# A depthwise convolution's taps, moved between two ways of feeding the matrix engine

## The reference

```
h = x + 0.5 * swiglu(rms(x), ffn1)
u = rms(h) @ w_in  ->  q, k, v, c, g
y_attn = window_attention(norm(q), norm(k), v, sink, rel_bias) @ w_attn_out
c = c_val * sigmoid(c_gate)                       # 512 channels
c = depthwise_conv(c, conv_w, conv_b)             # 31 taps along the tokens
c = silu(layer_norm(c));  y_conv = c @ w_conv_out
h = h + (sigmoid(g_a) * y_attn + sigmoid(g_c) * y_conv) @ w_o
h = h + 0.5 * swiglu(rms(h), ffn2);  x = h + (p @ w_pe_proj) * sigmoid(rms(h) @ w_pe_gate)
```

## Time and profile before

| | |
|---|---|
| three runs | 2152.19, 2153.51, 2154.12 us, median 2153.51 |
| the profiled execution | 2154.34 us, span 2152.5 us |
| TensorE busy | 2126.8 us, 99% of the span |
| VectorE busy | 1679.8 us, 78% |
| ScalarE busy | 1264.2 us, 59% |
| weight blocks | 664 of 512 KB |
| granted TensorE clock | 1.000 |

### The profile page before, as it was taken

One profiled execution on the slowest core, in us unless ns is written; L12 is line 12 of the kernel. 1 busy time (PEld: TensorE's weight loads), 2 busy tenths in 40 slices (PEclk: granted clock), 3 DMA queues, 4 the chain that ended last, 5 costly groups with the idle time before them and its releaser, 6 DMA issues.

```text
span 2152.5 us, 38861 instructions
## 1 busy us (share of the span) xinstructions
PE 2126.8 (99%) x16094; PEld 1940.7 (90%) x16094; DVE 1679.8 (78%) x2638; ACT 1264.2 (59%) x2114; POOL 13.4 (1%) x20
## 2 busy tenths in 40 slices
PE   8999999999999999999999999999999999999999
PEld 6898989999998899998888999888898889998888
DVE  7888699888877688776886677887688766978875
ACT  4755545555755655555655567666575645766554
POOL 0000000000000000000000000000000000000000
PEclk9999999999999999999999999999999999999999
DMA  9554476767644477555555533555555553345553
GB/s 365 198 194 168 162 252 251 246 233 278 225 155 173 148 245 236 190 183 186 182 190 187 176 118 128 202 190 187 190 180 187 189 190 131 120 166 205 190 191 129
DMA packets 116371, 415.12 MB, mean 193 GB/s; under 512 B 13105, under 2 KB 16561, under 8 KB 115682
## 3 DMA queue, kind: packets, MB, share of 16 engines
q1 hardware_dynamic: 116194, 412.63, 55.7%
HBM read 409.42 MB, written 3.16 MB: 192 GB/s over the span
## 4 chain that ended last, share of the span: by engine, by line
PE 91%; ACT 4%; DVE 3%; DMA 2%; issue 1%; SPq 0%; ACTq 0%; DVEq 0%
PE bank L198 90%; ACT arena L250 2%; DMA raw<-W 1%; DVE arena L205 1%; ACT hi L250 1%; DVE lo L205 1%; PE bank L202 1%; DVE ada L222 0%; ACT L250 0%; ACT L242 0%; DMA xT<-x 0%; DVE arena L213 0%; DVE h L205 0%; SPq L195 0%; DVE ysl L205 0%
## 5 line engine op out<-in xcount | busy, mean ns | idle before, releaser
L198 PE MATMUL bank<-h,hi 128*128 128x256 f32 (+1 forms) x5344 | 1223.1, 314 | 0.0
L250 ACT ACTIVATE hi<-raw 128x1024 fp32r<-128x1024 f32 x656 | 688.9, 1056 | 565.0 <-PE bank L198 501.5
L198 PE MATMUL bank<-h,lo 128*128 128x256 f32 x3440 | 986.1, 287 | 3.8 <-DVE h L205 3.7
L198 PEld LDWEIGHTS bank<-h,hi 128*128 128x128 f32 x5344 | 880.1, 190 | 67.1 <-issue 2.6
L205 DVE TENSOR_TENSOR lo<-raw,hi 128x1024 fp32r<-128x1024 f32 x656 | 793.1, 1221 | 90.4 <-ACT hi L250 89.7
L198 PEld LDWEIGHTS bank<-h,lo 128*128 128x128 f32 x3440 | 654.6, 190 | 15.6 <-issue 7.0
L198 PE MATMUL bank<-act,hi 128*128 128x512 f32 x1056 | 370.0, 393 | 0.0
L198 PE MATMUL bank<-act,lo 128*128 128x256 f32 x1056 | 294.7, 279 | 0.0
L198 PEld LDWEIGHTS bank<-act,hi 128*128 128x128 f32 x1056 | 197.9, 187 | 47.0
L198 PEld LDWEIGHTS bank<-act,lo 128*128 128x128 f32 x1056 | 197.9, 187 | 0.0
L250 ACT ACTIVATE arena<-arena 128x256 f32<-128x256 f32 (+4 forms) x202 | 98.6, 493 | 158.5 <-DVE arena L205 151.0
(11 more groups left out here) (150 smaller groups left out, 1894.0 us busy)
## 6 DMA issues: line engine op xcount, KB each, us to landing
raw<-W SPq DMA_DIRECT2D x664, 512.0 KB, 3.3
ada<-WA SPq DMA_DIRECT2D x80, 512.0 KB, 3.8
arena<-WA SPq DMA_DIRECT2D x16, 512.0 KB, 14.3
p_projected<-arena SPq DMA_DIRECT2D x2, 1024.0 KB, 7.5
arena<-scr SPq DMA_DIRECT2D x16, 128.0 KB, 4.9
arena<-p_projected SPq DMA_DIRECT2D x2, 1024.0 KB, 4.7
xT<-x SPq DMA_DIRECT2D x2, 512.0 KB, 5.2
arena<-lora SPq DMA_DIRECT2D x2, 512.0 KB, 9.6
```

Of the source, the lines that this page charges most:

```text
L198: return self.done(lambda e: e.matmul(out, l, r, start=start, stop=stop, skip_group_check=True))
L250: return self.done(lambda e: e.activation(out, in_, f, scale=scale, **kw))
```

## The change

The 44 float32 tap matmuls of a layer become 44 streamed tiles: each diagonal is laid out beforehand in the weight stream (5.5 more blocks a layer, 11 in all, 675 instead of 664), is split into high and low like any other tile, and makes three matmuls against the high part `Ch` and low part `Cl` of the convolution's input (266 columns, of which each tap reads 256 from its own offset). `tap halves` makes these copies: ScalarE `Ch`, VectorE `Cl`, channel tiles 0 and 1 ahead of c 3, tiles 2 and 3 behind gate2 2. The tiles of the first two channel tiles are a new item on TensorE behind rcol (a tiny item between c 3 and qkv), those of the other two follow gate2 3. ScalarE's building of diagonals goes. VectorE's 80 taps are spread over 24 ticks (4, 3, 3 and again) instead of 20, and one more empty tick stands ahead of the mean. On ScalarE the attention's chain, which ran behind the convolution's in a tick, now runs ahead of it.

```diff
-NT2 = 2 * (44 * 8 + 22 * 8) + 30 * 8 + 32 + 32 + 64 + 64 + 16
+NT2 = 2 * (44 * 8 + 22 * 8) + 30 * 8 + 32 + 32 + 64 + 64 + 16 + 4 * 11
 def conv2_steps(l):
-    s = []
+    s, n = [], 0
     for pair in (0, 2):
-        todo = [(m, j) for m in (pair, pair + 1) for j in range(CV, CW)]
-        built = []
-        for j in range(0, CV, 2):
-            s += [("taps", pair, j)]
-            if j >= 4:
-                s += [("pe tap", pair, *t) for t in built.pop(0)]
-            built.append(todo[:3])
-            del todo[:3]
-            s += [("diag", pair, *t) for t in built[-1]] + ["next"]
+        for size in (4, 3, 3) * 4:
+            s += [("taps", pair, n, n + size), "next"]
+            n += size
+        n = 0
         s += [("conv sum", pair)]
-    return s + ["next", ("mean",), "next", ("square",), "next", ("var",), "next", ("norm",), ("silu",), "next", ("split",)]
+    return s + ["next", "next", ("mean",), "next", ("square",), "next", ("var",), "next", ("norm",), ("silu",), "next", ("split",)]
...
-        s += [("mixer2", l), ("c", l, 0), ("c", l, 1), ("c", l, 2), ("conv2", l), ("c", l, 3), ("c last", l), ("rcol", l)]
+        s += [("mixer2", l), ("c", l, 0), ("c", l, 1), ("c", l, 2), ("conv2", l), ("tap halves", l, (0, 1)), ("c", l, 3),
+              ("c last", l), ("rcol", l), ("taps", l, 0)]
         s += [("qkv", l, p) for p in range(3)] + [("v2", l), ("qk norm", l), ("attention2", l)]
-        s += [("gate2", l, p) for p in range(8)] + [("gate2 last", l), ("finish", ("att2", l))]
+        s += [("gate2", l, p) for p in range(3)] + [("tap halves", l, (2, 3)), ("gate2", l, 3), ("taps", l, 2)]
+        s += [("gate2", l, p) for p in range(4, 8)] + [("gate2 last", l), ("finish", ("att2", l))]
...
+                elif what == "taps":
+                    l, pr = q
+                    o = take(CONV, ("conv", l, pr))
+                    for m in (pr, pr + 1):
+                        pe.wait_ge(v_cv, ("tap halves", l, m))
+                        for j in range(CV, CW):
+                            wh, wl, ends = tile([("conv_w_2", l, j, ("diag", m))])
+                            om = t256(o, m - pr)
+                            ch, cl = (x[m % 3][:, j - CV:j - CV + 256] for x in (Ch, Cl))
+                            pe.mm(om, wl, ch, j == CV, False)
+                            pe.mm(om, wh, ch, False, False)
+                            i = pe.mm(om, wh, cl, False, j == CW - 1)
...
+                        v.tt(Cl[m % 3], Cb[:, m, CV:CV + TW], Ch[m % 3].bitcast(F32), SUB).then_inc(v_cv, ("tap halves", l, m))
...
-                        a.act(diag[n % 8], C("ident"), ACT.Identity, scale=P("conv_w_2", l, j * 4 + m)).then_inc(
-                            a_cv, ("diag", l, m, j))
...
+                        a.act(Ch[m % 3], Cb[:, m, CV:CV + TW], ACT.Copy).then_inc(a_cv, ("tap high", l, m))
...
-                    f.chain(("att2", q[0]), att2_steps(q[0]), attention2(q[0]), True)
+                    f.chain(("att2", q[0]), att2_steps(q[0]), attention2(q[0]))
```

More of the change, by code:

```diff
@@ L1040, in conv2 @@
             def conv2(l):
-                taps = [0]
                 def step(what, *q):
-                    if what == "pe tap":
-                        pr, m, j = q
-                        if (m, j) == (pr, CV):
-                            take(CONV, ("conv", l, pr))
-                        d = diag[taps[0] % 8]
-                        taps[0] += 1
-                        pe.wait_ge(a_cv, ("diag", l, m, j))
-                        pe.wait_ge(v_main, ("c", l, m))
-                        pe.mm(t256(ps(("conv", l, pr)), m - pr), d, Cb[:, m, j:j + 256], j == CV, j == CW - 1).then_inc(
-                            pe_cv, ("tap", l, m, j))
-                    elif what == "mean":
+                    if what == "mean":
                         o = take(CONV, ("cmean", l))
@@ L1240, in tensor_program @@
                     f.chain(item, conv2_steps(q[0]), conv2(q[0]))
+                elif what == "taps":
[10 more added lines that the diff above has]
+                            i = pe.mm(om, wh, cl, False, j == CW - 1)
+                            names = ends + ([("conv", l, pr)] if (m, j) == (pr + 1, CW - 1) else [])
+                            if names:
+                                i.then_inc(pe_main, *names)
+                            if ends:
+                                f.tick()
                 elif what == "c":
@@ L1660, in step @@
                     if what == "taps":
[L1661 to L1671 removed]
+                        pr, first, last = q
+                        for n in range(first, last):
+                            j, m = n // 2, pr + n % 2
+                            o = t256(cacc, m)
+                            if j == 0:
+                                v.wait_ge(v_main, ("c", l, m))
+                                x = v.ts(o, Cb[:, m, 0:256], w(m, 0), P("conv_b_2", l, m), MUL, ADD)
+                            else:
+                                v.wait_ge(v_cv, ("tap", l, m, j - 1))
+                                x = v.stt(o, Cb[:, m, j:j + 256], w(m, j), o, MUL, ADD)
+                            x.then_inc(v_cv, ("tap", l, m, j))
                     elif what == "conv sum":
@@ L1674, in step @@
                         o = cacc[:, pr * 256:(pr + 2) * 256]
-                        v.wait_ge(pe_cv, ("tap", l, pr + 1, CW - 1))
+                        v.wait_ge(pe_main, ("conv", l, pr))
                         v.wait_ge(v_cv, ("tap", l, pr + 1, CV - 1))
@@ L1966, in vector_program @@
                     f.chain(item, conv2_steps(q[0]), conv2(q[0]))
+                elif what == "tap halves":
+                    l = q[0]
+                    for m in q[1]:
+                        v.wait_ge(a_cv, ("tap high", l, m))
+                        v.tt(Cl[m % 3], Cb[:, m, CV:CV + TW], Ch[m % 3].bitcast(F32), SUB).then_inc(v_cv, ("tap halves", l, m))
+                elif what == "taps":
+                    f.tiles(2 * (CW - CV))
                 elif what == "qkv":
@@ L2327, in conv2 @@
                 return step
-            conv_taps = [(m, j) for pr in (0, 2) for m in (pr, pr + 1) for j in range(CV, CW)]
             def merge(name, l, m, h):
@@ L2564, in scalar_program @@
                     f.chain(item, conv2_steps(q[0]), conv2(q[0]))
+                elif what == "tap halves":
+                    l = q[0]
+                    for m in q[1]:
+                        a.wait_ge(v_main, ("c", l, m))
+                        if m == 3:
+                            a.wait_ge(pe_main, ("conv", l, 0))
+                        a.act(Ch[m % 3], Cb[:, m, CV:CV + TW], ACT.Copy).then_inc(a_cv, ("tap high", l, m))
+                elif what == "taps":
+                    f.tiles(2 * (CW - CV))
                 elif what == "rcol":
```

27 lines of the change are left out of this document (5 added, 22 removed).

## The result

| | before | after |
|---|---|---|
| median of five runs each | 2153.62 us | 2162.14 us |
| lowest to highest | 2152.19 to 2154.12 | 2162.07 to 2162.97 |
| ratio, with its 95% interval | | 1.0040 [1.0030, 1.0051] |
| the profiled execution; its span | 2154.34; 2152.5 | 2162.12; 2160.3 |
| granted TensorE clock, mean | 1.000 | 0.998 |

The forecast was 2159.0, slower. The direction and the two large waits came out as laid out; two of the waits were smaller than their terms (2.9 us less together), and two costs for which the forecast had nothing, the clock and a wait at `attn out`, made up for it and more. That the total lies only 3 us off is so in part luck: the errors ran against each other.

What follows compares the result with a forecast made beforehand. TensorE, busy 99%, was taken as the bound: profiled 2154.3 - 5.9 (taps) - 1.0 (variance) + 12.4 (four turn waits) = 2159.8, or 2159.0 against the median. Own range 2156 to 2162; 8 in 10: 2147 to 2163.5.

Steps and rivals of the forecast that it cites:

- The taps: On TensorE, 88 float32 taps (37.6 us) become 88 streamed tiles at 0.36 us each (31.7): 5.9 us less.
- Turn 0: First attention transposes on TensorE would wait for ScalarE's scaling: 4.4 us in the first layer, 3.4 in the second.
- Turn 1: Second pair's attention transposes on TensorE would wait 2.1 us in the first layer, 2.5 in the second.
- Var: TensorE's 0.99 us wait at the convolution's variance would shrink to 0.5 per layer, saving 1.0 us in all.
- The clock: Rival, chance 0.10: TensorE's clock halves behind the two waits at turn 0, each costing 2.88 us more; 2165 us.
- no waits: Rival, chance 0.12: the attention's steps come in time, TensorE stays at 99%, gaining 5.9 plus 1.0; 2146.6 us.
- Half the wait: Rival, chance 0.12: exponentials, not VectorE's queue, decide at both reciprocals, leaving 6 to 7 us of waits; 2153 us.

Runs made afterwards that it cites:

- filler: Kernel after plus ten (first layer) and eight (second) matmuls on constants ahead of the wait at turn 0, result overwritten; 2162.53 us, 1.0036 to before.
- halves_early: Kernel after with the copies for channel tiles 2 and 3 made earlier, behind the second qkv item, turns unmoved; 2162.94 us, 1.0042 to before.
- early_filler: halves_early plus nine (first layer) and seven (second) filling matmuls on constants ahead of the wait at turn 0; 2159.46 us, 1.0028 to before.
- old_end: Kernel after with attention's chain last again on ScalarE and one empty tick, not two, ahead of the mean; 2160.68 us, 1.0032 to before.
- before_turn_earlier: Kernel before with one empty tick less between divide and turn, for both pairs; 2170.99 us, 1.0075 to before.
- no_float_taps: Kernel before without its 88 float32 taps and their diagonals, the sum adding a constant tile instead; 2132.39 us, 0.9898 to before.
- later_and_early: Kernel after with turns one tick later and second-pair copies made behind the second qkv item; 2151.68 us, 0.9990 to before.
- turn_later: Kernel after with one more empty tick between divide and turn, for both pairs; 2160.54 us, 1.0026 to before.
- table_moved: later_and_early with ScalarE's early table load moved from behind the square to right ahead of the variance's logarithm; 2148.93 us, 0.9977 to before.

## Why the forecast held, point by point

**The taps.** 0.36 us a tile, as the distance of high parts in the earlier trace rows had said; TensorE's busy time fell by 2.9 rather than 5.9; the slowed matmuls are counted in it, and the 3.0 missing agree with what the falls took. Nothing waited for the eleven added blocks.

**Turn 0: 4.4 and 3.4 forecast, 4.49 and 3.44 measured.** The two sums from one common point, 29.5 and 25.1, came out at 29.82 in all and 29.82 - 4.49 = 25.33 for TensorE; in the second layer, for 29.9 and 26.5, at 30.22 and 30.22 - 3.44 = 26.78. What made this work is that the queue of VectorE was laid out row by row in its new order, taps and low parts included, rather than the chain's own operations alone.

**Turn 1: 2.1 and 2.5 forecast, 0.84 and 0.85 measured.** The sum was off in two ways. TensorE took 25.04 us from turn 0 to turn 1 and not 23.1, since part of it ran at 1.2 GHz; filler, with the clock up, has 24.94 - 1.49 = 23.45. VectorE's and ScalarE's side was 24.94 there, for 25.2, so with the clock up the forecast's terms nearly hold, and the waits were 1.5 and 1.9. In the kernel after that side took 25.88, and it is not VectorE's queue that decides at the second reciprocal, as the forecast had it. VectorE stands there for ScalarE's exponentials, and the high part ahead of these had stood for TensorE:

```profile
1300.48 1.06 ACT L251 ACTIVATE hi<-raw 128x1024 fp32r<-128x1024 f32 x1 [2.51 <-PE bank L199]
```

```profile
1305.61 0.17 DVE L206 TENSOR_TENSOR sml<-sml 128x8 f32<-128x8 f32 x1 [0.57 <-ACT arena L251]
```

In the second layer these are 2.53 and 0.21. A later TensorE so makes the other side later too, and the wait stays at 0.85: from scores 1 to turn 1 it is 19.5 us in both layers of after, halves_early and early_filler, and 20.15 in filler's first, where VectorE's queue decides.

**Var: 0.5 forecast, 0.56 measured.** But old_end shows that the order on ScalarE, to which the forecast gave the gain, isn't its cause.

**The clock: a rival at 10%, partly true.** It fell behind both long waits, 3.4 us in all. The rival had 5.8, one whole plain tick at 1.2 GHz for each. Its condition, a wait of more than 3.4 us, which I took from the one wait in the earlier trace rows, is wrong: the runs have falls behind 1.92 and 1.97. And that one wait could not have shown that the clock holds, since it stands at the start of the program, ahead of TensorE's first work:

```profile
3.39 3.75 PE L198 MATMUL bank<-crow,cst 1*128 1x512 f32 x4 [3.39 <-ACT crow L250]
```

Four matmuls of 512 columns take 3.75 us there, where six take 2.31 in the earlier trace rows. This was the largest cost that the forecast's sum had put at nothing.

**Attn out: not laid out, 1.24.** The forecast had said that a wait might come up at a place it didn't cover. It looked at ScalarE's new order, but in the first layer, and not at the table's load in the second, where the stream stands half a block later.

**The sum.** From 2154.3: taps -5.9, turns +9.6 (for 12.4), var -0.9 (for -1.0), attn out +1.2, clock +3.4: +7.5 of the measured 7.8 (+7.1 with the eighth off the clock). By landmarks on TensorE (the tiny rcol matmuls start at 1226.61 and 1792.16 before, at 1225.93 and 1795.30 after) the first layer grew by 3.8 (3.7 by the ledger) and all from the second rcol on by 4.7 (3.9); what lies ahead of the first was 0.7 shorter. The last 0.8 us behind the second rcol I can't place.

Of the rivals, no waits is refuted by the rows at the turns. Half the wait is refuted at turn 0; its condition, the exponentials and not VectorE's queue at the reciprocal, was met at turn 1. That the attention's distance in ticks and not the streamed tile is what costs is shown from both sides, by before_turn_earlier and no_float_taps.

## What to carry to other kernels

Where dependent steps are counted in ticks of a stream, making the ticks shorter is an edit of every such distance: work out each chain's time against its new number of ticks, and move the reader by a tick where it is late, together with whatever else stands behind the same slow step (later_and_early, -10.5 us against the kernel after). A step that is counted at a fixed block must be looked at in every layer, since half a block's shift changes what stands beside it. When TensorE is the bound, add to each new wait of about 2 us or more what the clock may take behind it, here 1.4 to 2.9 us by the sum.

## What the runs showed of the hardware

**The clock falls behind a standstill, but not always behind one of the same length.** The granted clock behind TensorE's waits, and what the fall took by the sum of (1 - clock) x time:

| wait (us) | runs | fell, us taken |
|---|---|---|
| 4.49 | after, old_end, halves_early | 1.7, 1.7, 2.9 |
| 4.26 | no_float_taps, twice | 2.4, 1.5 |
| 4.04, 3.64 | turn_later | 2.7, 1.6 |
| 3.80, 3.81 | before_turn_earlier | 2.7, 1.4 |
| 3.44, 3.44, 3.45 | after, old_end, halves_early | 1.7, 1.5, none |
| 1.97, 1.98 | before_turn_earlier | 1.7, none |
| 1.92, 1.61, 1.49 | filler, later_and_early, filler | 1.7, none, none |

The longest of these stretches, the microseconds from turn 0 on in halves_early:

```profile
1284.50:1290.00 5.50, 5.50 (x26) 5.50 (x27) 3.39 (x7) 4.80 (x8) 0.00 (x0) 0.50 0.01 3
```

TensorE was busy through all 5.5 us at 1.2 GHz. Two neighbouring tiles there (only the last row of each is shown) are 0.64 us apart, for 0.36 at 2.4 GHz:

```profile
1288.16 0.63 PE L199 MATMUL bank<-h,hi 128*128 128x256 f32 x2
...
1288.80 0.63 PE L199 MATMUL bank<-h,hi 128*128 128x256 f32 x2
```

Part of why the cost differs from fall to fall at like waits is that the clock can fall while TensorE still stands: in halves_early it was down from about 1283.4 us, and the wait ended at 1284.50. The time down inside a wait costs nothing.

The Trainium skill, "TensorE: Matmul & The Clock Gate", section "What's actually happening", ties the halved clock to idle time; the traces agree that it follows idle time and comes back by itself under work, but the length of the wait alone doesn't tell whether it falls: 3.44 and 3.45 went different ways, and so did 1.97 and 1.98.

**Keeping TensorE at work holds the clock.** In early_filler and filler the transposes behind 3.2 to 4.5 us of filling matmuls ran at 2.4 GHz. It holds only there: in filler the clock fell at the next wait, 1.92 us.

**A table load is repeated when another function comes between.** Logarithm and exponential shared one load where no tanh stood between it and them (table_moved, old_end, before), and took one each, 1.28 us, where one did (after, second layer).
